# Order of the work at the entry of the feed-forward layers, and the odd attention's stream bias as bf16 rows added by TensorE

## What is computed

```python
for l in range(2):
    x = x + 0.5 * swiglu(rmsnorm(x, norm_g[l, 0]), ffn_w_gu[l, 0], ffn_w_down[l, 0])
    x = x + mixer(rmsnorm(x, norm_g[l, 1]))          # even, then odd
    x = x + 0.5 * swiglu(rmsnorm(x, norm_g[l, 2]), ffn_w_gu[l, 1], ffn_w_down[l, 1])
# swiglu: g, u = split(x @ w_gu);  (silu(g) * u) @ w_down

def fox_sample(q, k, v, logf, ck, cv, clogf):        # the streams, over 1024 cached rows
    fq = jnp.cumsum(logf, axis=1)
    c_after = lax.cumsum(clogf, axis=1, reverse=True) - clogf
    fk = jnp.concatenate([-c_after, fq], axis=1)
    s = jnp.einsum('bihd,bjhd->bhij', q, concat(ck, k)) * (D ** -0.5)
    s = s + fq[..., :, None] - fk[..., None, :]      # the row's own term drops out of the softmax
    p = jax.nn.softmax(where(valid, s, -inf));  return p @ concat(cv, v)
```

## Time and profile before

| what | value |
|---|---|
| median of 3 runs | 2693.63 us (2692.27 to 2693.68) |
| the profiled execution, its own time | 2691.87 us |
| its span in the trace | 2690.0 us |
| mean granted TensorE clock | 0.971 |
| PE busy / DVE / ACT / POOL | 95% / 61% / 36% / 29% |
| read from / written to HBM | 279.95 MB / 21.41 MB |

### The profile page before, as it was taken

The page is one execution under the profiler, slowest core; times in us unless marked ns, Lnnn a source line. Parts: engine busy times, 40 slices in busy tenths (PEclk is TensorE's granted clock), DMA queues, the critical chain, the costliest instruction groups (busy, mean ns, idle before and its releaser), DMA issues.

```text
span 2690.0 us, 45814 instructions
## 1 busy us (share of the span) xinstructions
PE 2550.0 (95%) x18803; PEld 2409.7 (90%) x18803; DVE 1637.6 (61%) x2438; ACT 955.5 (36%) x1493; POOL 785.3 (29%) x434
## 2 busy tenths in 40 slices
PE   7999999999789999999899999999888898999997
PEld 7999999998659999999899999999844488999997
DVE  7777587222446968488877758721133349685675
ACT  5333242220264424243433324221055444243341
POOL 1322323331151232323232332332133341323232
PEclk8999999999699999999999999999989999999998
DMA  3222222222361222222222222225699931222221
GB/s 112 71 87 87 87 71 88 79 69 108 114 228 48 69 89 86 88 79 73 70 67 91 86 83 76 88 98 145 226 356 370 366 139 48 80 86 79 87 79 71
DMA packets 79223, 304.16 MB, mean 113 GB/s; under 512 B 10769, under 2 KB 18722, under 8 KB 64050
## 3 DMA queue, kind: packets, MB, share of 16 engines
q1 hardware_dynamic: 79026, 301.39, 33.0%
HBM read 279.95 MB, written 21.41 MB: 112 GB/s over the span
## 4 chain that ended last, share of the span: by engine, by line
PE 79%; DVE 9%; DMA 5%; issue 3%; ACT 2%; POOL 1%; DVEq 0%; SPq 0%; ACTq 0%; POOLq 0%
PE ps L382 34%; PE ps L869 33%; PE ps L1258 4%; DMA kv_ring<-in_fox_kc 4%; DMA kv_ring<-in_fox_vc 1%; PE ps L1580 1%; PE ps L1614 1%; DVE wb_lo L706 1%; PE ps L1539 1%; PE ps L1554 1%; DVE gate_prod L1076 1%; POOL w_lo L368 1%; PE ps L1595 1%; DVE w_raw L672 1%; PE ps L1565 1%
## 5 line engine op out<-in xcount | busy, mean ns | idle before, releaser
L869 PE MATMUL ps<-xs_hi,wb_hi 128*128 128x320 f32 x2112 | 659.6, 312 | 24.1 <-POOL wb_lo L755 12.7
L869 PE MATMUL ps<-xs_hi,wb_lo 128*128 128x320 f32 x2112 | 655.7, 310 | 0.0
L869 PE MATMUL ps<-xs_lo,wb_hi 128*128 128x320 f32 x2112 | 655.5, 310 | 0.0
L368 POOL TENSOR_TENSOR w_lo<-w_raw,w_hi 128x1024 fp32r<-128x1024 f32 (+2 forms) x130 | 398.6, 3067 | 612.7 <-ACT w_hi L364 612.7
L755 POOL TENSOR_TENSOR wb_lo<-w_raw,wb_hi 128x512 fp32r<-128x512 f32 x176 | 268.7, 1531 | 962.1 <-PE ps L869 777.4
L869 PEld LDWEIGHTS ps<-xs_hi,wb_hi 128*128 128x128 f32 x2112 | 399.3, 189 | 28.0 <-POOL wb_lo L755 13.4
L869 PEld LDWEIGHTS ps<-xs_lo,wb_hi 128*128 128x128 f32 x2112 | 399.5, 189 | 1.0 <-issue 1.0
L869 PEld LDWEIGHTS ps<-xs_hi,wb_lo 128*128 128x128 f32 x2112 | 399.3, 189 | 0.0
L364 ACT ACTIVATE w_hi<-w_raw 128x1024 fp32r<-128x1024 f32 (+2 forms) x130 | 158.3, 1217 | 647.7 <-PE ps L382 511.5
L382 PE MATMUL ps<-h_hi,w_hi 128*128 128x320 f32 x1408 | 322.1, 310 | 3.4 <-DVE h_lo L1070 3.4
L382 PE MATMUL ps<-h_hi,w_lo 128*128 128x320 f32 x1408 | 320.8, 309 | 0.0
(11 more groups left out here) (242 smaller groups left out, 4312.6 us busy)
## 6 DMA issues: line engine op xcount, KB each, us to landing
w_raw<-in_w_up SPq DMA_DIRECT2D x175, 512.0 KB, 4.4
kv_ring<-in_fox_kc SPq DMA_DIRECT2D x32, 1024.0 KB, 13.4
kv_ring<-in_fox_vc SPq DMA_DIRECT2D x32, 1024.0 KB, 13.0
w_raw<-in_w_down_a SPq DMA_DIRECT2D x64, 384.0 KB, 3.1
w_raw<-in_w_in SPq DMA_DIRECT2D x24, 1024.0 KB, 4.8
w_raw<-in_w_down_b SPq DMA_DIRECT2D x32, 512.0 KB, 3.5
fox_s_s<-s_bias_dram SPq DMA_DIRECT2D x16, 576.0 KB, 10.0
kv_ring<-in_band_kc SPq DMA_DIRECT2D x8, 1024.0 KB, 6.9
```

What stands on the lines that cost most here:

```text
L368: nc.gpsimd.tensor_tensor(out=w_lo[:, slot, 0:cols], in0=w_raw[:, slot, 0:cols], in1=w_hi[:, slot, 0:cols].bitcast(F32), op=ALU.subtract). ...
L869: last = nc.tensor.matmul(ps[:, bank, 0:HALF], w_part[:, slot, cols], x_part[:, k, :], start=k == 0 and i == 0, stop=k == 3 and i == 2)
```

## The change

Two changes at once.

**Feed-forward layers.** (1) The last three steps of `acc_dve` (blocks 5, 6, 7) and ACT's last square go from the end of the phase before into tile 0 of the layer; `ffn_stats` goes from after P4 of tile 0 to after P2 of tile 1. (2) `two_hi_step` stands ahead of `sums_act` at the last unit. (3) POOL's low part A22 of tile t waits for `pair_lo` of tile t+1 (not in tile 0 and not in a group's last tile; tile 0 waits for P3 where it waited for P6), and A11 of the next tile has no wait for P7 any more. (4) In tile 1 the `rs` chain comes after `sum_last`; in tile 2 the steps of gates and hidden values have another order. (5) `SLOTS` is P3, P7, P6, P4 in its second half.

**Odd attention.** `c_after` and the own `neg_f` are cut into three bf16 parts by ten DVE instructions in the projection (`c_parts`, `own_parts`), and SP stores these (`s_rows_dram`, 768 KB, and `own_rows_dram`) in place of `s_bias_dram`. For a unit SP loads 24 rows of 1024 bf16 (three loads of 16 KB); for the own keys three small loads serve all units. PE multiplies them with `row_heads`, a 24 x 128 matrix of 0 and 1 that repeats each head's row for its 16 frames, into the PSUM bank of the logits ahead of the keys' products: three more bf16 matmuls for each unit. DVE's instruction stays, with a zero in place of the bias. `row_heads` is made at the start from three loads of 1024 single elements each.

```diff
-SLOTS = ("P1", "P2", "P5", "X", "P3", "P4", "P7", "P6")
+SLOTS = ("P1", "P2", "P5", "X", "P3", "P7", "P6", "P4")
...
@@ plain_lo_step @@
         if at_count:
             pool.wait_ge(product_done, at_count)
+        if pairs:
+            pool.wait_ge(pair_lo, pairs)
@@ ffn_pe @@
-                    if (t, name) == ((0, "P4") if ph["norm"] else (1, "P2")):
+                    if (t, name) == (1, "P2"):
                         ffn_stats(pe, ph)
@@ ffn_pool @@
-                plain_lo_step(pool, ph, t, "A22", done_at(ph, t, "P6"))
+                plain_lo_step(pool, ph, t, "A22", done_at(ph, t, "P6" if t else "P3"),
+                              up_at(ph, t)[0] + 2 if 0 < t < hi - 1 else 0)
                 if t + 1 < hi:
-                    plain_lo_step(pool, ph, t + 1, "A11", done_at(ph, t, "P7"))
+                    plain_lo_step(pool, ph, t + 1, "A11")
@@ ffn_dve @@
-                if t == 1 and ph["norm"]:
-                    ffn_norm_dve(dve, ph)
+                if t == 2:
+                    dve.wait_ge(inv_ready, 2 * (ph["index"] + 1))
+                    gate_part(0)
                 if more:
                     sum_two(dve, ph, t + 1)
...
                 if more:
                     sum_last(dve, ph, t + 1)
+                if t == 1:
+                    ffn_norm_dve(dve, ph)
...
                 if more:
                     pair_lo_step(dve, ph, t + 1)
+                if t == 0 and ph["norm"]:
+                    acc_dve(dve, 5, 5, sq_before(ph))
+                    acc_dve(dve, 6, 6, sq_before(ph))
@@ the phase before, its last unit @@
                     if last:
                         sums_lo_dve(dve, nxt, d)
-                        for m in (5, 6, 7):
-                            acc_dve(dve, m, m, sq_base)
@@ load_sample_bias @@
+            if self.masked:
...
+                    if n >= 2:
+                        sp.wait_ge(self.slogits_ready, n - 1)
+                for part in range(3):
+                    sp.dma_start(self.tiles["s_rows"][n % 2][8 * part:8 * part + 8, :],
+                                 s_rows_dram[part, 8 * n:8 * n + 8, :]).then_inc(self.sbias_loaded[n % 2], 16)
+                return
@@ s_logits @@
+                    if self.masked:
+                        if ch == 0:
+                            pe.wait_ge(self.sbias_loaded[n % 2], 48 * (n // 2 + 1))
+                        nc.tensor.matmul(ps[:, 4 + ch, 0:512], row_heads[0:24, :],
+                                         self.tiles["s_rows"][n % 2][:, 512 * ch:512 * ch + 512], start=True, stop=False)
                     pe.wait_ge(self.ring_loaded[r], loaded)
@@ fgate_dve, after the copy of c_after @@
+            for rest, parts in ((neg_f[:, SEQ:], own_parts), (c_after[:, :], c_parts)):
+                for part in range(3):
+                    if part:
...
+                        nc.vector.tensor_tensor(out=rest, in0=rest, in1=parts[:, part - 1, :],
+                                                op=ALU.subtract).then_inc(f_parts, 1)
...
+                    nc.vector.tensor_copy(parts[:, part, :], rest).then_inc(f_parts, 1)
@@ sync @@
-                for b in range(DEC_BATCH):
-                    sp.dma_start(s_bias_dram[b * H_C:(b + 1) * H_C, :, PAST:],
-                                 neg_f[:, SEQ:].unsqueeze(1).broadcast_to([H_C, DEC_SEQ, P])).then_inc(f_scratch, 16)
...
-                sp.dma_start(s_bias_dram[:, 0:half, 0:PAST], repeated).then_inc(f_scratch, 16)
+                sp.wait_ge(f_parts, 10)
+                sp.dma_start(own_rows_dram.rearrange("p h c -> h p c"), own_parts[:, :, :]).then_inc(f_scratch, 16)
+                sp.dma_start(s_rows_dram.rearrange("p r c -> r p c"), c_parts[:, :, :]).then_inc(f_scratch, 16)
```

115 lines of the change are left out of this document (77 added, 38 removed).

## The result

The changed kernel takes 2668.14 us (median of 3 runs, 2666.59 to 2668.65) where the kernel before takes 2693.63; the ratio is 0.9908 with a 95% interval of 0.9892 to 0.9923. That is 25.5 us less; I had forecast 31 less, 2662.6, with a range of 2647 to 2683. The profiled execution took 2666.59, its span is 2664.8.

A forecast was written before the change was run, and what follows sets the result against it. PE was taken as the bound in steady feed-forward tiles, DMA in the fox stage, with PE waits at layer entries. From 2691.87 us, less 13 (feed-forward) and 18 (fox), 2660.9; plus 1.8 for the median, 2662.6, range 2647 to 2683.

The forecast's parts named there:

- 18 us: Fox stage: gain from smaller bias loads less the added PE products, with ends of 8 and 26 us.
- two chains so close do not hide in each other wholly: Fox stage: with DMA and PE bounds nearly equal, PE's 21.3 and 8.3 us waits for keys and values partly remain.
- 12.8 for the three later layers: Feed-forward entries: forecast gains of 4.5 us in the second layer, 4.1 in the third and 4.2 in the last.
- With the squares moved, L672 can start at 2240.99, ahead of GpSimd: Last layer's entry: VectorE's sums avoid GpSimd, 2.59 us earlier, 1.07 and 0.99 shorter, together 4.65.
- The sum 2.59 + 1.07 + 0.99 - 1.78 = 2.9: Last layer's entry: L1129 comes 2.9 us earlier after two squares come back ahead of it.
- longest wait, 2.6: Last layer's entry: PE's longest wait, taken as the one for L1129, was to go as that comes 2.9 us earlier.
- The sum of 3 to 5 us: Last layer's entry, as a sign: PE's waits for L1129 and L720 sum to this in place of 8.2.
- 1.7 forecast: First layer's entry: gain of 1.7 us from the order of tile 2 and the low parts alone.
- 1.5, inside the 0 to 10: Steady feed-forward tiles: loss of 1.5 us, range 0 to 10, from the closed loop of slab load and A22.
- a loop that is too long, a little: Rival, steady tiles: loop 0.4 to 0.6 us longer than the tile costs 10 to 20 us; about 2676; chance 0.16.
- the same loop on the other side: Rival, steady tiles: loop reaching 13.3 us loses 39 us against 31 gained; about 2702 us; chance 0.05.
- The projection and the start: 0: Odd projection's ten VectorE instructions cost 0, else 7 us; the start's three small loads 0, else some 3 us.

The follow-up runs named there:

- e3: Changed kernel, but in the second and third tile group of each feed-forward layer GpSimd's A22 and A11 wait for P6 and P7 as before; 2664.5 us.
- e4: Changed kernel with two of the three sums of squares back at the end of the phase before the three later feed-forward layers; 2666.9 us.
- e12: Changed kernel run again unchanged, to see how executions of one program differ; 2670.0 us.
- e2: Kernel before with the odd attention's part of the change alone; 2678.2 us.
- e5: Changed kernel with ScalarE's `two_hi_step` put back behind `sums_act` at the last unit of phases ending in a feed-forward layer; 2677.2 us.
- e8: Changed kernel, but GpSimd's A22 of tile 0 waits for P6 as before, not P3; 2669.4 us.
- e10: Changed kernel with the new GpSimd waits only at tiles 1 and 2; from tile 3 A22 waits for P6 and A11 for P7 as before; 2660.9 us.
- e11: Changed kernel with GpSimd's old waits in the second and third tile groups and two squares back in the phase before; 2667.1 us.
- e9: Kernel before with only `two_hi_step` moved ahead of `sums_act` at the last unit of phases ending in a feed-forward layer; 2688.1 us.
- e6: Changed kernel without the three bf16 bias-row products per unit, so the streams' logits lack their bias; transfers the same; 2672.0 us.
- e7: Changed kernel with each of the 32 wide bf16 bias-row products made twice; transfers the same; 2673.8 us.

## Why the prediction was right, and where not

**The fox stage: right, and by the reasons given.** I took 18 us between the bounds of DMA (19.3 to 22.5 less) and PE (20 less). The trace has 17.6, or 18.8 without a stretch at half clock at the projection's start. The stage moved 74.66 MB, as said, and took 212 us from its first load to the point at which the earlier trace rows end it, as said; wide products cost 0.215 each. I had expected PE to wait 10 to 15 us for keys and values, it was 5.0. The claim that "two chains so close do not hide in each other wholly" did not come true in this trace, and does in others, as the spread of 12 to 21 us shows: with the same code PE waits 5 us for loads in four traces (this one, e3, e4, e12) and 7 to 13 in five (e2, e5, e8, e10, e11), and e5 has two more stretches at half clock. So 17.6 is so near to 18 partly by luck: with the same code 12.2 to 20.8 were possible. The conditions written for being wrong, a stage over 222 us or waits for `bias_rows`, did not come.

**The rate of the stage.** By the Trainium skill ("DMA: Bandwidth & Descriptors", "Where 436 GB/s comes from") the limit of 358 GB/s would be the stage's rate. In the middle of the changed stage the rate is 358, which agrees; but it is PE that is without gaps there, and e12's stretch of 165 us in the middle of its stage ran at 366, as before the change whole slices ran at 420. So here it is no limit for a slice, and these runs don't decide whether it is one for the mean.

**The entries: 8.7 in place of 12.8 for the three later layers.** The step that failed is the first: "With the squares moved, L672 can start at 2240.99, ahead of GpSimd: 2.59 earlier, 1.07 shorter, and L681 0.99 shorter". The first sum starts 7.8 us after tile 0 does (2213.91 and 2206.13), where it was 12.5. But I assumed that GpSimd's pair stays where it was, and it came forward as far: its condition is P3 now, it starts 7.4 us after tile 0 in place of 12.0, and the sums take 1.79 and 2.21 as before. The step left out of the working was to ask what releases the pair. So the terms 1.07 and 0.99 came to nothing. The sum 2.59 + 1.07 + 0.99 - 1.78 = 2.9 was for L1129; the last layer has 2.67 for the squares moved away, -1.75 for the two that come back, -0.29 for the wait of L1149 for them, 0.6 in all, and e5 shows 0.55. The 2.6 that L1154 is in fact earlier, counted from tile 0, hold 2.0 that were not in the sum: L733's wait for ScalarE. What the prediction doesn't name, the order on ScalarE, is 6 of the 8.7 us (e5, e9). e4 shows that moving two of the squares gains nothing, e8 that moving GpSimd's pair off the sums gains nothing either.

Two more things were read or left out wrongly. The "longest wait, 2.6" of the earlier trace rows is not the one behind the L1129 of the earlier trace rows: that one is 1.5, and the 2.6 stands in tile 3. And with the waits of tile 0 gone and `ffn_stats` in tile 1, PE now waits 3.3 in one piece at P5 of tile 1, with half clock behind it. The sum of 3 to 5 us that I gave for the waits for VectorE holds; its place and the clock were not forecast. Of the other terms, GpSimd's A22 at tile 3 came as said (1.2; forecast 1.25) and the 0.8 at `h_lo` went; the 1.0 at P4 of tile 1 did not come. P5 of tile 3 is 3.0 us earlier in the last layer (forecast 3.5), P5 of tile 5 2.5 (forecast 3.25).

**The first layer: 1.7 forecast, 3.6 seen, and these are not its own.** It is the time at which the full clock comes. The changed kernel's first trace and e4, e6 and e7 have it early, e3, e5, e8 and e12 2.5 to 3.5 us later and e10 and e11 1.4, with the same code up to there but for GpSimd's condition in tile 0 of e8. A late one is 0.2 us ahead of the kernel before at tile 1, and 0.5 (e3) or 1.2 (e12) at tile 6. Between these two tiles the changed kernel's first trace gains nothing, e12 1.0; the 1.7 that I had worked out are not there. The waits for `part` of the earlier trace rows did go, but at 40 to 114 us there stands in their place

```profile
PE ps L884 <- POOL wb_lo L770: 3.0, 3, 1.6
```

so what the forecast for this layer doesn't name is GpSimd's A22, ahead of P4 of tiles 1, 2 and 3.

**The steady tiles: right mechanism, cost 4.5 in place of 1.5, inside the 0 to 10.** The loop is as long as the tile, as worked out from its rows, and in the steady tiles, but for the second of each group, a slab's sum now starts 0.02 us after its landing. What I mis-sized is the scatter: not a mean that is too long, but single slabs that come 6.1 to 7.0 us after A22's end in place of 4.9 to 5.7, five in this trace, cost 0.4 to 1.5 us of PE each (4.3 of the 4.5). e3 gives back 4.5. The rival "a loop that is too long, a little" happened at less than half of its price; the same loop on the other side did not.

**The projection and the start: 0, as said.** VectorE's ten instructions end at 1850.8, the next piece of keys is taken right behind them, and PE has no wait in what is left of the projection; the casts to bf16 took 0.69 us, less than the 1.2 that I had put for them. The second tile's slab landed at 23.6 behind the three small loads, 4.2 later than before and still 10 ahead of its first use.

**The sum.** -8.7 - 17.6 - 3.6 + 4.2 is -25.7 in the trace; what else moved, up to 1.5 us either way in the mixers, the output projection and the last norm, comes to 0.5, so that the span is 25.2 shorter. The forecast was -31. Without the start the change's own gain in this trace is nearer 22; e12's median ratio, 0.9916, points to the same.

## What to carry to other kernels

A helper engine's start is not a fixed point: before counting on a step slipping in ahead of it, find what releases the helper, and whether that comes forward too. When a wait makes a buffer's release depend on the work on the next buffer, add up the loop and compare it with the period; if they are equal, the mean loses nothing but each late landing is paid, and the wait belongs only where it is needed (by e10's one trace, here tiles 1 and 2 of 22). Count how far a point moved, and not only how long the wait at it is: here one wait of 3.3 took the place of one of 1.5 though its releaser came 2.6 us earlier. Where two bounds have come together, expect little from relieving one, and read no gain from a single trace: here the stage spread by 8.6 us over nine kernels with one code, and by 2.7 over three with the old one.

## What the runs showed of the hardware

The granted clock makes two executions of one program differ at the same place by 3.3 us at the start. The fox stage differs by up to 8.6 us in kernels with the same code there; PE's waits for loads in it are 5 us in the four shortest of the nine traces and 7 to 13 in the other five. Behind PE's wait of 2.8 to 3.4 us in tile 1 the granted clock is 0.5 for 3.4 us in most of the traces, for 6.8 in some and not at all in others (third layer of e8 and e12). A VectorE instruction with two SBUF operands beside GpSimd's subtraction is held by 1.0 to 1.1 us for each of GpSimd's when it begins soon after it (0.68 to 1.79, 1.23 to 2.21, 1.22 to 2.31), whichever it is, and by less, 0.46, when GpSimd's ends 0.6 us later. Beside VectorE's reads from PSUM GpSimd took 1.28 us each (2.56 for two) where it had taken 1.5 before.
